# A two-layer encoder with expert-choice MoE on one core: GpSimd's arrival at a barrier, the order of the weight loads and one add in the routing

## The reference

```python
def expert_choice_ffn(h, router, w_gate, w_up, w_down):
    ...
    aff = jax.nn.softmax((xt @ router).astype(jnp.float32), axis=-1)
    gate, idx = lax.top_k(aff.T, cap)
    xe = xt[idx]
    hid = jax.nn.silu(jnp.einsum('ecd,edf->ecf', xe, w_gate)) * jnp.einsum('ecd,edf->ecf', xe, w_up)
    ye = jnp.einsum('ecf,efd->ecd', hid, w_down) * gate[..., None].astype(h.dtype)
    out = jnp.zeros_like(xt).at[idx.reshape(-1)].add(ye.reshape(-1, D))
    return out.reshape(Bn, S, D)
```

## Time and profile before

| | |
|---|---|
| median of 3 runs | 2428.69 us |
| the profiled execution's own time | 2428.31 us |
| its span | 2426.5 us |
| TensorE matmul busy | 2224.6 us (92%) |
| VectorE busy | 1469.1 us (61%) |
| ScalarE busy | 1288.8 us (53%) |
| GpSimd busy | 341.9 us (14%) |
| mean granted clock of TensorE | 0.957 |
| moved by DMA | 503.78 MB, mean 208 GB/s |

### The profile page before, as it was taken

The page is one execution under the profiler, slowest core; times in us unless marked ns, Lnnn a source line. Parts: engine busy times, 40 slices in busy tenths (PEclk is TensorE's granted clock), DMA queues, the critical chain, the costliest instruction groups (busy, mean ns, idle before and its releaser), DMA issues.

```text
span 2426.5 us, 33580 instructions
## 1 busy us (share of the span) xinstructions
PE 2224.6 (92%) x11896; PEld 1694.3 (70%) x11896; DVE 1469.1 (61%) x2055; ACT 1288.8 (53%) x1621; POOL 341.9 (14%) x252
## 2 busy tenths in 40 slices
PE   4998989998949999999997999999976999999997
PEld 3787885556836777777765887888764777777774
DVE  3223124545377988898884223233456898889886
ACT  4323143545236677777765334323424777677774
POOL 1000023000001122212203213211000112211210
PEclk9998999999969999999998999999887999999998
DMA  3211113000179999999982101110039999999993
GB/s 129 84 47 31 53 32 121 22 22 0 70 292 341 390 383 384 388 392 382 383 314 100 43 25 58 41 30 1 26 141 357 376 380 383 389 392 383 383 392 143
DMA packets 139596, 503.78 MB, mean 208 GB/s; under 512 B 14935, under 2 KB 23511, under 8 KB 136196
## 3 DMA queue, kind: packets, MB, share of 16 engines
q1 hardware_dynamic: 132292, 477.39, 51.5%
q0 software_dynamic: 6944, 24.38, 4.5%
q10 hardware_dynamic: 288, 1.05, 0.1%
HBM read 472.77 MB, written 31.52 MB: 208 GB/s over the span
## 4 chain that ended last, share of the span: by engine, by line
PE 74%; issue 11%; DVE 6%; ACT 2%; POOL 2%; POOLq 1%; DMA 0%; DVEq 0%; ACTq 0%; SPq 0%
PE proj_ps L1989 15%; PE pT_ps L1989 15%; PE score_ps L1989 15%; PE proj_ps L725 9%; PE proj_ps L1681 4%; PE proj_ps L715 3%; PE o_ps L450 2%; PE score_ps L427 2%; PE score_ps L582 2%; PE o_ps L605 1%; PE proj_ps L1654 1%; PE pT_ps L438 1%; POOL arena L1480 1%; PE pT_ps L593 1%; PE o_ps L2025 1%
## 5 line engine op out<-in xcount | busy, mean ns | idle before, releaser
L1975 DVE TENSOR_TENSOR w_lo<-arena,w_hi_more 128x2048 fp32r<-128x2048 f32 x192 | 431.2, 2286 | 123.1 <-ACT w_hi_more L1971 123.1
L1975 DVE TENSOR_TENSOR w_lo<-arena,w_hi 128x2048 fp32r<-128x2048 f32 x192 | 433.0, 2284 | 36.3 <-ACT w_hi L1971 19.3
L1971 ACT ACTIVATE w_hi<-arena 128x2048 fp32r<-128x2048 f32 x192 | 355.8, 1905 | 21.4 <-PE proj_ps L1989 12.3
L1971 ACT ACTIVATE w_hi_more<-arena 128x2048 fp32r<-128x2048 f32 x192 | 356.1, 1903 | 14.4 <-POOLq L271 14.4
L739 ACT ACTIVATE arena<-proj_ps 128x512 f32<-128x512 f32 (+5 forms) x84 | 43.2, 514 | 321.1 <-PE proj_ps L725 278.4
L1989 PE MATMUL proj_ps<-w_lo,x_hi 128*96 128x512 f32 x512 | 162.1, 398 | 0.0
L1989 PE MATMUL pT_ps<-w_lo,h_hi 128*96 128x512 f32 x512 | 161.6, 397 | 0.0
L1989 PE MATMUL score_ps<-w_lo,x_hi 128*96 128x512 f32 x512 | 159.8, 393 | 0.0
L741 DVE COPY arena<-proj_ps 128x256 f32<-128x256 f32 (+5 forms) x44 | 22.5, 511 | 176.6 <-PE proj_ps L725 174.3
L532 ACT ACTIVATE arena<-arena,nmax 128x256 f32<-128x256 f32 (+5 forms) x216 | 98.3, 457 | 45.1 <-DVE nmax L483 44.2
L427 PE MATMUL score_ps<-arena 128*128 128x256 f32 (+5 forms) x432 | 101.6, 365 | 20.8 <-DVE arena L741 10.1
(11 more groups left out here) (234 smaller groups left out, 4989.9 us busy)
## 6 DMA issues: line engine op xcount, KB each, us to landing
arena<-w_gate SPq DMA_DIRECT2D x128, 1024.0 KB, 8.3
arena<-w_up SPq DMA_DIRECT2D x128, 1024.0 KB, 8.1
arena<-w_down SPq DMA_DIRECT2D x128, 1024.0 KB, 6.6
aT<-w_a SPq DMA_DIRECT2D x12, 1024.0 KB, 4.9
arena<-w_c SPq DMA_DIRECT2D x12, 1024.0 KB, 4.8
arena<-w_out SPq DMA_DIRECT2D x2, 4096.0 KB, 15.8
residual_rows<-x SPq DMA_DIRECT2D x12, 512.0 KB, 2.7
arena<-residual_rows SPq DMA_DIRECT2D x6, 1024.0 KB, 7.2
```

Of the source, the lines that this page charges most:

```text
L1971: act.activation(self.hi(run, i), self.raw[:, slot], ACT.Copy).then_inc(self.w_hi, 1)
L1975: dve.tensor_tensor(self.lo(run, i), self.raw[:, self.raw_slot(run, i)], self.hi(run, i).bitcast(F32), ALU.subtract).then_inc(self.w_lo, 1)
```

## The change

Three edits. GpSimd's step of the routing phase moves into `arrived`: GpSimd arrives at the phase's barrier first, then waits for the lists, starts the first gather and waits for the other engines. In `sp_first`, SP waits before the load with index 6 until the first expert's gather has landed, so loads 6 to 11 (two up slabs of the first expert and the gate slabs of the second) come behind it. In `Middle.dve`, the add of the last half tile stands behind round 4 of the prompt's search instead of round 5, and VectorE's turn and inversion of that tile behind round 5 instead of round 6. All three hold in both layers.

```diff
                 self.dve_turned(dve, 4)
-                self.dve_top(dve, 0, range(3, 6))
+                self.dve_top(dve, 0, range(3, 5))
                 self.dve_add(dve, 5, 1)
-                self.dve_top(dve, 0, range(6, 7))
+                self.dve_top(dve, 0, range(5, 6))
                 self.dve_turned(dve, 5)
                 self.dve_invert(dve, 5)
-                self.dve_top(dve, 0, range(7, 8))
+                self.dve_top(dve, 0, range(6, 8))
...
                     for i in range(2 * NS):
+                        if i == 6:
+                            sp.wait_ge(self.gathered, 16 * NE * l + 16)
                         self.load(sp, "first", NE * l, i, first=(l == 0))
...
-                       "mid0": [mids[0].pool], "moe0": [experts.pool(0), mix_c.pool_early], "c": [mix_c.pool],
-                       "mid1": [mids[1].pool], "moe1": [experts.pool(1)]},
-                {"moe0": [tails[0].pool_lo]})
+                       "moe0": [experts.pool(0), mix_c.pool_early], "c": [mix_c.pool],
+                       "moe1": [experts.pool(1)]},
+                {"mid0": [mids[0].pool], "moe0": [tails[0].pool_lo], "mid1": [mids[1].pool]})
```

## The result

The changed kernel takes 2408.47 us (median of 4 runs, 2407.43 to 2409.51) against 2428.89 us; the ratio is 0.9915, 95% interval 0.9898 to 0.9933. The interval means a gain of 16.3 to 24.8 us, so 16.6 lies at its lower edge. Its profiled execution took 2409.51 us, with a span of 2407.7.

A forecast was written before the change was run, and what follows sets the result against it. Bound: TensorE, 74% of the path, with winnable idle time where GpSimd's gather drain and VectorE's remainders run serially. Gains of 8.3 us per layer, 16.6, from 2428.31 gave 2411.7, plus 0.4 for the median: 2412.1; range 2408.7 to 2420.5.

The forecast's parts named there:

- The seams: Between routing stage and experts, both layers: first gate matmul starts 8.3 us earlier in each, 16.6 in all.
- today's landing: First gather of each layer lands 8.2 and 7.5 us after issue, as before; kept unchanged, gains total 14.6 us.
- two bounds: Gather's landing at the seam: as before gives 14.6 us gain, at the shortest, 4.8 us, gives 18.5.
- Part 1: Routing-stage barrier: GpSimd arrives before its gather, moving layer 0's release from 707.02 to about 699.6 by itself.
- Part 2: Top-8 search: the add moves up one round, lists come 2.27 us earlier, VectorE's 2.31 us wait nearly goes.
- Part 3: SP's loads 6 to 11 wait for the gather, leaving only loads 0 to 5's tail beside it; cost nothing.
- the floor: Seam strand of barrier release plus VectorE's 6.70 us of weight remainders: gains 9.6 and 8.9, in all 18.5 us.
- Rival A: Seam: gather's DMA instruction slips behind one VectorE remainder, costing 2.1 us a layer, 2418.3; chance 0.23 including longer landings.
- Rival B: Seam: GpSimd is shut out for all three VectorE remainders, so nothing is won, 2429 us; chance 0.07.
- rival C: First experts: weight stream becomes the bound, up to 3.5 us later per layer, 2435.7 us; chance 0.04.
- What follows a first matmul moves with it rigidly, as TensorE sets the pace.: After each layer's first gate matmul: later work keeps its duration, so the seams' 16.6 us is the whole gain.

The follow-up runs named there:

- the copies: Changed kernel with one or two small GpSimd copies of the index list, with waits, ahead of the first gather: 2410.27 and 2407.99 us.
- the fills: Matmuls with overwritten results added in TensorE's idle time; two of them per layer put into the changed kernel gave 2406.59 us.
- the filled pair: Kernel before with TensorE's idle time filled by extra matmuls, 2425.01 us, and changed kernel with its idle time filled likewise, 2404.36 us.
- three fills: Changed kernel plus matmuls behind the barrier, before the first gate and before the turn of the first hidden rows: 2402.97 us, again 2404.36.

## Why the prediction was wrong, point by point

**The seams: right.** The forecast was 8.3 and 8.3 us, 16.6 in all; 8.56 and 7.91 were measured, 16.47 in all, and again 8.59 and 8.00. Part of that is luck: the one microsecond off today's landing was a guess between two bounds, and 1.2 and 0.6 were measured. (What the prediction calls VectorE's turn of the rows is its gain on the rows that TensorE has turned.) Step by step, layer 0's times of the changed kernel being 1.27 us later from the untouched start on:
- Part 1. The barrier was to open at 697.4, with ScalarE as the last; it opened at 698.32, 697.05 without the later start, by ScalarE.
- Part 2. The wait of 2.31 us is gone, and the lists come 2.30 us earlier against the end of the projection (18.61 us behind it instead of 20.91), for 2.27 in the forecast.
- Part 3. The landing was taken as 7.2 and 6.5 us and measured 7.03 and 6.94; load 5, to land at 703.7 and so to start ScalarE's sixth split, starts it at 704.42. Nothing held back was missed.
- The gather is last and not the floor, as the forecast's value had it.

**Rival A fell** as a cost: the gather's DMA instruction still takes 1.13 us, although the remainders start half-way into it (697.67 and 698.32). So the rule quoted there, that whoever starts first has the port, is borne out by the trace on its first half alone: GpSimd started first. What it costs at the seam when it starts second was not tried, since the copies did not delay it; in the expert loop the gather of 3.04 us started at 786.50, 0.07 us behind a remainder. **Rival B** fell with it, and **rival C**: ScalarE's splits do wait for loads (1.89 us ahead of the sixth), but off the path, and the first products are shorter than before.

**The step that failed** is the sentence "What follows a first matmul moves with it rigidly, as TensorE sets the pace." TensorE sets the pace, but not at one pace. The same products take 36.6 us at the full clock and took 40.1 and 40.3 in before, 39.3 in the changed kernel, 37.9 to 40.4 in the other versions without fills. What falls at 1.2 GHz behind an idle stretch changed with the kernel: of the 3.60 us behind the first gate matmuls that the forecast lacked, 1.83 are in the first products, where the fills show them to be clock. The other 1.77 us (1.26 and 0.51) lie in stretches of untouched work; the trace puts 1.57 of them into two places where the same matmuls ran under a lower granted clock in before, and no run of its own tried them. Ahead of the first seam 1.27 us were lost in work that the change does not reach, which leaves 2.33 us beyond the seams in the profiles. The 1.6 us more in the medians stand in no trace; the runs of one kernel spread further than that. The Trainium skill, page "TensorE: Matmul & The Clock Gate", section "Part 1: The HAM clock gate (the "warmup" mystery)", says that the number of slow matmuls differs from run to run of one kernel, with the gate's phase at the kernel's start. The trace agrees: the first gate and its turn took 11.77 us in one execution of one kernel and 13.34 in another.

The range was too narrow for the same reason. Its lower end was the seams' floor less 1.5 us for the runs' spread; the clock moves the rest of the span by more than that with nothing changed at the seams, 2404.7 to 2410.1 us over the four profiles of kernels that share the changed kernel's seams. A range of the seams' bounds widened by 4 us on either side would have held the time.

**Still open.** Before and changed repeat their profiles to 0.5 us, and their medians lie 20.4 and 20.7 apart in two sets. Whether the gain beyond the seams belongs to this change or to where its work happened to fall under the clock is not settled: of the two versions with copies, whose seams are nearly the same, one has a span 2.4 us longer and one a span 3.0 us shorter than the changed kernel's, and the filled pair leaves it open, since its medians (20.6) and its profiles (17.3 or 11.7) disagree.

**A faster version.** The changed kernel with three fills has the lowest medians, 2402.97 and 2404.36 us, ratios 0.9895 and 0.9904; its intervals overlap with that of the changed kernel, so 3.5 to 5.5 us are likely and not certain. Holding two loads more beside the fills gave the fastest single runs (2395.6) but no better median.

## What to carry to other kernels

GpSimd, which arrived at a barrier with a gather in flight, made everyone wait for the landing, since its arrival drains it (8.57 us): let such an engine arrive first and let the one reader wait for the transfer's own semaphore. Six 1 MB loads that nobody needed yet cost a small gather beside them about 1 us of landing here, and two more another 2.5, so hold such loads back until it has landed. When you forecast from a chain of waits, cost the stretch you change by the chain, but give the untouched work behind it a band of its own for TensorE's clock, and judge an experiment by the stretch in its profile and not by the median alone.

## What the runs showed of the hardware that was not expected

- A gather of 96 rows of 4 KB lands 4.1 to 4.8 us after its issue beside the tail of four loads, 6.8 to 7.7 beside that of six, and 7.5 to 8.6 among twelve, over all versions.
- On GpSimd, one or two copies of 0.18 us with a wait cost less time ahead of a gather than a bare semaphore increment there: 0.54 and 0.79 us from the list to the gather's instruction, against 0.94.
- One kernel's executions lay 13.4 us apart (2396.02 and 2409.43) with seams equal to 0.3 us; mean clocks 0.967 and 0.963.
